# Attention visits of TensorE re-sequenced in a one-core decoder layer

## The chip, the cores and the metric

One core of one Trainium2 chip runs the whole layer. The time is device microseconds (us) of that core, from launch to end; smaller is better. The clock of TensorE has two levels, 1.2 and 2.4 GHz, and the profile gives the granted share of the higher one.

## The reference, cut to what matters

One layer on 512 tokens of width 1024: adaLN modulation of an RMSNorm, a mixture of three dilated sliding-window attentions with 16 heads of 64, a gated ConvFFN with a width-3 causal convolution, and a final RMSNorm.

```python
def reference(x, c, ...):
    mod = silu(c) @ w_ada + b_ada
    sh1, sc1, g1, sh2, sc2, g2 = split(mod, 6)
    h = rms_norm(x, norm_mix) * (1 + sc1) + sh1
    qkv = (h @ attn_w_in).reshape(B, S, 3, 3, 16, 64)        # q,k,v x groups x heads
    for g, (window, dilation) in enumerate(((128, 1), (512, 4), (2048, 16))):
        o, lse = dilated_window_attention(q[g], k[g], v[g], window, dilation)
    o = sum(softmax(lses over g) * outs)                     # a mixture per head
    x = x + g1 * (o @ attn_w_out)
    h = rms_norm(x, norm_ffn) * (1 + sc2) + sh2
    x = x + g2 * conv_ffn(h, w_up, conv_w, conv_b, w_down)
    return rms_norm(x, norm_final)
```

## The kernel before, in words

All large products are made in fp32r with operands split in a high and a low part (wh, wl for weights; hh, hl for the input): three matmuls of 128x512 for each 128 rows of contraction. ScalarE (ACT) makes the high part of a weight strip (L883), VectorE (DVE) the low part (L1131).

Attention goes by pairs of heads, of which there are 8. TensorE (PE) runs `body(n, par, project, attend)` nine times. With `project` it makes the nine q/k/v strips of pair n (L604 to L606), and with `attend` the attention of pair n-1. Body 0 only projects, bodies 1 to 7 do both (three rounds of a loop of two, and one more), body 8 only attends. A body has 18 half strips, h = 0 to 17, of 12 matmuls each; between them stand the visits to other work, at the h that a table gives:

- `make_scores` (L609) makes query-key products for a quarter d of the scores: side 0 (d = 0, 1) is the first group in windows of two blocks (L621), side 1 (d = 2, 3) the other two groups (L628). Contraction is over 64 rows, so head 0 uses the upper and head 1 the lower half of the array's rows, and the heads alternate matmul by matmul. Both heads write their own one of the two `score` banks. `mask_scores` on DVE (L1202) adds the mask, takes the maximum and moves them to `probs`, ACT exponentiates in place (L953).
- `turn_values` (L633) and `turn_probs` (L651) are transposes against the identity (L641, L657) into the two `turn` banks; DVE copies bank 0 out and ACT bank 1 (`take_turn`, L1192 and L923). `sum_ada` (L648) turns a partial sum of the modulation in bank 1 of the same pair; the counter `turn_taken` orders all of them.
- `weigh_values` (L661) makes the value products of one unit u: head u % 2 and quarter j = u // 2. Its weights are 64 columns wide, and head 0 writes partitions 0 to 63 of an output bank `o_acc[side]`, head 1 partitions 64 to 127. A visit makes a quarter: all of head 0's 6 or 8 matmuls, then all of head 1's (L676).

The tables put scores at h = 0, 2, 4, 6, the turned values at 3, 5, 7, the modulation sum at 10, the turned probabilities at 12, 14, 15, 16 and the value products at 14, 15, 16, 17. Between scores and probabilities DVE mixes the three groups' softmax denominators (h = 8, 9) and scales `probs` (`weigh`, L1218). At the end of a body ACT copies the output bank (L966), DVE adds the two (L1294), and ACT and DVE split the sum (L970, L1299).

In body 8 there is no projection; in its place PE begins the output projection (L684 to L686), `FILL_AT` giving the number of steps of three matmuls at each h. The last step of each of these four strips waits for the last pair's low part (L750). Then follow the rest of the output projection and the ConvFFN, which the change doesn't touch.

Of the kernel before, what the change touches and what calls it, by code (L numbers as in the profile page):

```python
# [25 lines left out]
P = 128  # L26
# [4 lines left out]
H, E = 16, 64  # L31
# [44 lines left out]
def decoder_layer(nc, x, c, w_ada, b_ada, norm_mix, norm_ffn, attn_w_in, attn_w_out,  # L76
# [11 lines left out]
    with ctx:  # L88
# [113 lines left out]
        turned = [sem("turned0"), sem("turned1")]  # L202
        turn_taken = [sem("turn_taken0"), sem("turn_taken1")]
# [18 lines left out]
        def turns_before(n):  # L222

            return 0 if isinstance(n, int) and n == 0 else 6 * n - 4


        SCORE_AT = {0: 0, 2: 1, 4: 2, 6: 3}
# [3 lines left out]
        TURN_P_AT = {12: 0, 14: 1, 15: 2, 16: 3}  # L231
        PV_AT = {14: 0, 15: 1, 16: 2, 17: 3}
# [7 lines left out]
        FILL_AT = {1: 3, 3: 3, 5: 3, 7: 10, 12: 3, 14: 1, 15: 1, 17: 4}  # L240
# [41 lines left out]
        def qkv_slot(n, s):  # L282
            return RING if is_first(n) and s == RING else s % RING

# [255 lines left out]
        def _(pe):  # L540
# [68 lines left out]
            def make_scores(n, par, d):  # L609
# [3 lines left out]
                pe.wait_ge(masked, 4 * (n - 1) + d + 1)  # L613
                side, tiles = d // 2, (2 * (d % 2), 2 * (d % 2) + 1)
                for b in tiles:
                    at = HALF * (b % 2)
                    if side == 0:
                        lo = P * max(b - 1, 0)
                        for hd in range(2):
                            e = slice(E * hd, E * (hd + 1))  # L620
                            last = nc.tensor.matmul(score[hd][:, at + (P if b == 0 else 0):at + HALF],  # L621
                                                    q_t[e, par, 0, P * b:P * (b + 1)],
                                                    k_t[e, par, 0, lo:P * (b + 1)], start=True, stop=True)
                    else:
                        for g in (1, 2):
                            for hd in range(2):
                                e = slice(E * hd, E * (hd + 1))
                                last = nc.tensor.matmul(score[hd][:, at + P * (g - 1):at + P * g],  # L628
# [874 lines left out]
```

## Time and profile before

| what | value |
|---|---|
| runs | 1020.44, 1021.26, 1022.64 us (median 1021.26) |
| profiled execution: span, first to last instruction | 1017.7 us |
| median of the runs less that span | 3.56 us |
| PE matmul busy | 973.8 us, 96% |
| DVE, ACT busy | 514.6 us (51%), 403.3 us (40%) |
| granted TensorE clock, mean | 0.988 |
| value products L676 | 480 matmuls, 47.1 us busy |
| scores L628, L621 | 384 matmuls, 35.1 us busy |
| turned probabilities L657 | 240, 33.0 us busy |

The profile is of one execution, and gives its span; what lies around it is known only as the distance to the median of the runs. A matmul's duration overlaps its neighbours' (the pipeline), so what a matmul costs PE is the distance from its start to the next one's start, which the timeline shows.

### The profile page before, as it was taken

The numbers are of one execution on the slowest core, as the hardware profiler recorded it, in microseconds if no ns is written. First come the engines' busy times: TensorE is split into PE (matmuls) and PEld (weight loads), VectorE is DVE, ScalarE is ACT, GpSimd is POOL, SyncE is SP. The second block draws the span as 40 slices with busy tenths as digits, with TensorE's granted clock in tenths as the row PEclk, the third lists the DMA queues.
The fourth block names the chain that finished last, engine by engine and source line by source line (L and its number), as shares of the span: only waits on it lengthen the run. The fifth ranks groups of instructions, "written<-read, shape, count | busy, mean of one in ns | idle before, by whom it ended". The sixth has DMA issues, their size and how long they took to land.

```text
span 1017.7 us, 14215 instructions
## 1 busy us (share of the span) xinstructions
PE 973.8 (96%) x5008; PEld 784.4 (77%) x5008; DVE 514.6 (51%) x1115; ACT 403.3 (40%) x721; POOL 31.3 (3%) x43
## 2 busy tenths in 40 slices
PE   4589999999999999999999989999999999999996
PEld 3478787887877878878778779888888888888885
DVE  5863663655735646357365557644444444412214
ACT  7433443434435344353443534633333333321212
POOL 3500000000000000000000000100000000000000
PEclk9699999999999999999999999999999999999999
DMA  9746341432324314333232203333333323232212
GB/s 310 210 116 194 112 133 48 125 118 90 95 89 123 124 41 124 124 103 124 62 114 74 62 22 90 100 101 91 95 97 89 102 83 103 83 104 86 99 62 83
DMA packets 151533, 106.94 MB, mean 105 GB/s; under 512 B 3510, under 2 KB 138830, under 8 KB 151502
## 3 DMA queue, kind: packets, MB, share of 16 engines
q1 hardware_dynamic: 151296, 106.45, 34.4%
q8 instruction: 19, 0.31, 0.1%
q14 instruction: 12, 0.10, 0.0%
q10 hardware_dynamic: 206, 0.08, 0.0%
HBM read 104.42 MB, written 2.10 MB: 105 GB/s over the span
## 4 chain that ended last, share of the span: by engine, by line
PE 92%; DVE 5%; ACT 1%; issue 1%; DMA 1%; SPq 0%; DVEq 0%; POOL 0%; ACTq 0%
PE bank L604 13%; PE bank L606 13%; PE bank L605 13%; PE bank L797 8%; PE bank L798 8%; PE bank L799 8%; PE bank L676 4%; PE bank L822 4%; PE bank L821 4%; PE bank L823 4%; PE bank L657 3%; PE bank L628 2%; PE bank L621 1%; DVE acc L1093 1%; PE bank L684 1%; PE bank L686 1%
## 5 line engine op out<-in xcount | busy, mean ns | idle before, releaser
L1131 DVE TENSOR_TENSOR wl<-raw,wh 128x1024 fp32r<-128x1024 f32 x144 | 177.4, 1232 | 305.1 <-ACT wh L883 304.6
L883 ACT ACTIVATE wh<-raw 128x1024 fp32r<-128x1024 f32 x144 | 152.2, 1059 | 200.8 <-PE bank L799 112.9
L604 PE MATMUL bank<-hh,wl 128*128 128x512 f32 x552 | 227.0, 411 | 0.0
L606 PE MATMUL bank<-hl,wh 128*128 128x512 f32 x552 | 218.7, 396 | 0.0
L605 PE MATMUL bank<-hh,wh 128*128 128x512 f32 x552 | 218.3, 395 | 0.0
L799 PE MATMUL bank<-fl,wh 128*128 128x512 f32 x336 | 133.0, 396 | 0.0
L798 PE MATMUL bank<-fh,wh 128*128 128x512 f32 x336 | 133.0, 396 | 0.0
L797 PE MATMUL bank<-fh,wl 128*128 128x512 f32 x336 | 133.0, 396 | 0.0
L604 PEld LDWEIGHTS bank<-hh,wl 128*128 128x128 f32 x552 | 104.1, 189 | 27.8 <-issue 5.7
L606 PEld LDWEIGHTS bank<-hl,wh 128*128 128x128 f32 x552 | 103.9, 188 | 24.7
L605 PEld LDWEIGHTS bank<-hh,wh 128*128 128x128 f32 x552 | 104.1, 189 | 20.7
L953 ACT ACTIVATE probs<-probs,nmax 128x256 f32<-128x256 f32 (+1 forms) x128 | 61.9, 485 | 98.4 <-DVE nmax L1208 98.4
L797 PEld LDWEIGHTS bank<-fh,wl 128*128 128x128 f32 x336 | 63.2, 188 | 15.3
L799 PEld LDWEIGHTS bank<-fl,wh 128*128 128x128 f32 x336 | 63.2, 188 | 15.2
L798 PEld LDWEIGHTS bank<-fh,wh 128*128 128x128 f32 x336 | 63.2, 188 | 15.1
L822 PE MATMUL bank<-act_h,wh 128*128 (+1 forms) x160 | 63.4, 396 | 0.0
L823 PE MATMUL bank<-act_l,wh 128*128 (+1 forms) x160 | 63.4, 396 | 0.0
L821 PE MATMUL bank<-act_h,wl 128*128 (+1 forms) x160 | 63.3, 396 | 0.0
L1192 DVE COPY p_t<-bank 128x512 f32<-128x512 f32 x32 | 22.1, 690 | 61.7 <-PE bank L657 61.7
L923 ACT ACTIVATE p_t<-bank 128x512 f32<-128x512 f32 x32 | 19.1, 598 | 79.4 <-PE bank L657 79.4
L676 PEld LDWEIGHTS bank<-p_t,v_n 128*64 128x64 f32 x480 | 39.4, 136 | 12.0 <-issue 10.7
L676 PE MATMUL bank<-p_t,v_n 128*64 128x128 f32 x480 | 47.1, 279 | 0.3 <-DVE p_t L1192 0.3
(175 smaller groups left out, 1147.7 us busy)
## 6 DMA issues: line engine op xcount, KB each, us to landing
raw<-in_attn_w_in SPq DMA_DIRECT2D x72, 512.0 KB, 3.8
raw<-in_ffn_w_up SPq DMA_DIRECT2D x44, 512.0 KB, 3.8
ada_raw<-in_w_ada SPq DMA_DIRECT2D x16, 1024.0 KB, 5.7
raw<-in_ffn_w_down SPq DMA_DIRECT2D x22, 512.0 KB, 3.3
ada<-in_w_ada SPq DMA_DIRECT2D x16, 256.0 KB, 7.1
raw<-in_attn_w_out SPq DMA_DIRECT2D x8, 512.0 KB, 3.6
x_nat<-in_x SPq DMA_DIRECT2D x4, 512.0 KB, 5.2
x_nat<-in_w_ada SPq DMA_DIRECT2D x8, 256.0 KB, 6.3
```

Source lines behind the costliest of these rows:

```text
L604: nc.tensor.matmul(bank[:], wl[:, slot, t], xh[:, t], start=(t == 0), stop=False)
L605: nc.tensor.matmul(bank[:], wh[:, slot, t], xh[:, t], start=False, stop=False)
L606: last = nc.tensor.matmul(bank[:], wh[:, slot, t], xl[:, t], start=False, stop=(t == KT - 1))
L676: last = nc.tensor.matmul(o_acc[side][e, P * b:P * (b + 1)], values, p_t[:, u % PT_RING, P * i:P * (i + 1)], start=first, stop=final)
L797: nc.tensor.matmul(bank[:], wl[:, slot, t], fh[:, t], start=(t == 0), stop=False)
L798: nc.tensor.matmul(bank[:], wh[:, slot, t], fh[:, t], start=False, stop=False)
L799: last = nc.tensor.matmul(bank[:], wh[:, slot, t], fl[:, t], start=False, stop=(t == KT - 1))
L821: nc.tensor.matmul(y[:], wl[:, slot, o], xh, start=start, stop=False)
L822: nc.tensor.matmul(y[:], wh[:, slot, o], xh, start=False, stop=False)
L823: last = nc.tensor.matmul(y[:], wh[:, slot, o], xl, start=False, stop=False)
L883: nc.scalar.activation(dst, src, ACT.Copy).then_inc(done, 1)
L1131: nc.vector.tensor_tensor(dst, src, high.bitcast(F32), ALU.subtract).then_inc(done, 1)
```

## The change

The scores of a side are made in one visit, its second quarter in the `turn` banks. Masks and exponentials get a table of their own (`MASK_AT`). The value products come in two visits, at h = 14 and 16, with the two heads alternating matmul by matmul. The probabilities of a side are turned in one visit over four banks (`turn` and `score`), in body 8 still quarter by quarter over two. The values are turned in the output banks. DVE scales the second half of `probs` at h = 11, ahead of its first copy of turned probabilities. The output steps in body 8 are spread anew, and each kind of turning has semaphores of its own.

```diff
-        SCORE_AT = {0: 0, 2: 1, 4: 2, 6: 3}
+        SCORE_AT = {0: (0, 1), 4: (2, 3)}
+        MASK_AT = {0: 0, 1: 1, 4: 2, 5: 3}
         TURN_V_AT = {3: 0, 5: 1, 7: 2}
         ADA_READ_AT = {0: 0, 1: 1, 2: 2, 3: 3, 5: 4, 6: 5, 7: 6, 8: 7}
         ADA_AT = 10
-        TURN_P_AT = {12: 0, 14: 1, 15: 2, 16: 3}
-        PV_AT = {14: 0, 15: 1, 16: 2, 17: 3}
+        TURN_P_AT = {12: (0, 1), 14: (2, 3)}
+        TURN_P_LAST = {12: (0,), 13: (1,), 14: (2,), 15: (3,)}
...
...
         def qkv_slot(n, s):
             return RING if is_first(n) and s == RING else s % RING
+        def score_bank(d, hd):
+            return (score, turn)[d % 2][hd]
+        def turn_bank(u, project):
...
                 if d == 0:
                     pe.wait_ge(strip_taken, STRIPS * n)
-                pe.wait_ge(masked, 4 * (n - 1) + d + 1)
+                if d == 1:
+                    pe.wait_ge(ada_taken, n)
...
-                            last = nc.tensor.matmul(score[hd][:, at + (P if b == 0 else 0):at + HALF],
+                            last = nc.tensor.matmul(score_bank(d, hd)[:, at + (P if b == 0 else 0):at + HALF],
...
             def turn_values(n, par, g):
                 k, use = g % 2, g // 2
                 pe.wait_ge(strip_taken, STRIPS * n + g + 1)
-                if not (isinstance(n, int) and n == 0 and use == 0):
-                    pe.wait_ge(turn_taken[k], turns_before(n) + use)
+                if use:
+                    pe.wait_ge(v_taken[0], 2 * n + 1)
+                elif not is_first(n):
+                    pe.wait_ge(o_summed, n)
                 src = v_t[:, (par + g) % 2]
                 for b in range(NT):
                     keys = src[:, P * b:P * (b + 1)] if g == 0 else src[:, b:T:4]
-                    last = nc.tensor.transpose(turn[k][:, P * b:P * (b + 1)], keys, ident[:])
-                last.then_inc(turned[k], 1)
+                    last = nc.tensor.transpose(o_acc[k][:, P * b:P * (b + 1)], keys, ident[:])
+                last.then_inc(v_turned[k], 1)
             def sum_ada(n):
                 pe.wait_ge(acc_step, KT * (n + 1))
-                pe.wait_ge(turn_taken[1], turns_before(n) + 1)
+                if not is_first(n):
+                    pe.wait_ge(masked, 4 * n)
                 for j in range(NT):
                     last = nc.tensor.transpose(turn[1][:, P * j:P * (j + 1)], acc[:, P * j:P * (j + 1)], ident[:])
-                last.then_inc(turned[1], 1)
-            def turn_probs(n, u, before):
-                hd, j, k = u % 2, u // 2, u % 2
+                last.then_inc(ada_turned, 1)
+            def turn_probs(n, u, project):
+                hd, j = u % 2, u // 2
                 pe.wait_ge(scaled, 8 * (n - 1) + u + 1)
-                pe.wait_ge(turn_taken[k], turns_before(n) + before + j)
+                if project and u == 1:
+                    pe.wait_ge(ada_taken, n + 1)
+                ring = 2 if project else 1
+                if j >= ring:
+                    pe.wait_ge(p_taken[hd], 4 * (n - 1) + j - ring + 1)
                 for i, (b, part) in enumerate(p_blocks(j)):
-                    last = nc.tensor.transpose(turn[k][:, P * i:P * (i + 1)],
+                    last = nc.tensor.transpose(turn_bank(u, project)[:, P * i:P * (i + 1)],
                                                probs[:, hd, j // 2, b, P * part:P * (part + 1)], ident[:])
-                last.then_inc(turned[k], 1)
-            def weigh_values(n, par, u, before):
-                hd, j, k = u % 2, u // 2, u % 2
-                e = slice(E * hd, E * (hd + 1))
-                pe.wait_ge(turn_taken[k], turns_before(n) + before + j + 1)
-                if u == 0:
+                last.then_inc(p_turned[hd], 1)
+            def weigh_values(n, par, j, project):
+                for hd in range(2):
+                    pe.wait_ge(p_taken[hd], 4 * (n - 1) + j + 1)
+                if j == 0:
                     pe.wait_ge(o_summed, n)
+                    if project:
+                        pe.wait_ge(v_taken[0], 2 * n + 2)
+                        pe.wait_ge(v_taken[1], n + 1)
                 side = j // 2
                 blocks = p_blocks(j)
                 for i, (b, part) in enumerate(blocks):
-                    if side == 0:
-                        values = v_n[:, par, 0, b - 1 + part, e]
-                    else:
-                        values = v_n[:, par, 1 + part, b, e]
                     first = i == 0 or blocks[i - 1][0] != b
                     final = i == len(blocks) - 1 or blocks[i + 1][0] != b
-                    last = nc.tensor.matmul(o_acc[side][e, P * b:P * (b + 1)], values, p_t[:, u % PT_RING, P * i:P * (i + 1)],
-                                            start=first, stop=final)
+                    for hd in range(2):
+                        e = slice(E * hd, E * (hd + 1))
+                        if side == 0:
+                            values = v_n[:, par, 0, b - 1 + part, e]
+                        else:
+                            values = v_n[:, par, 1 + part, b, e]
+                        last = nc.tensor.matmul(o_acc[side][e, P * b:P * (b + 1)], values,
+                                                p_t[:, (2 * j + hd) % PT_RING, P * i:P * (i + 1)],
+                                                start=first, stop=final)
...
-                            pe.wait_ge(masked, 4 * PAIRS + 1)
+                            pe.wait_ge(masked, 4 * PAIRS)
...
                         if h in SCORE_AT:
-                            make_scores(n, 1 - par, SCORE_AT[h])
-                        if h in PV_AT:
-                            for u in (2 * PV_AT[h], 2 * PV_AT[h] + 1):
-                                weigh_values(n, 1 - par, u, before)
-                        if h in TURN_P_AT:
-                            for u in (2 * TURN_P_AT[h], 2 * TURN_P_AT[h] + 1):
-                                turn_probs(n, u, before)
+                            for d in SCORE_AT[h]:
+                                make_scores(n, 1 - par, d)
+                        for j in PV_AT.get(h, ()):
+                            weigh_values(n, 1 - par, j, project)
+                        for j in (TURN_P_AT if project else TURN_P_LAST).get(h, ()):
+                            for u in (2 * j, 2 * j + 1):
+                                turn_probs(n, u, project)
                     if attend and not project and h in FILL_AT:
                         begin_out(fill_steps[filled:filled + FILL_AT[h]])
...
-            def take_turn(n, use, dst):
-                act.wait_ge(turned[1], turns_before(n) + use + 1)
-                nc.scalar.activation(dst, turn[1][:], ACT.Copy).then_inc(turn_taken[1], 1)
+            def take_probs(n, j, project):
+                act.wait_ge(p_turned[1], 4 * (n - 1) + j + 1)
+                u = 2 * j + 1
+                nc.scalar.activation(p_t[:, u % PT_RING], turn_bank(u, project)[:], ACT.Copy).then_inc(p_taken[1], 1)
...
                         if (TURN_V_FIRST if is_first(n) else TURN_V_AT).get(h) == 1:
-                            take_turn(n, 0, v_n[:, par, 1].rearrange("p b e -> p (b e)"))
+                            act.wait_ge(v_turned[1], n + 1)
+                            nc.scalar.activation(v_n[:, par, 1].rearrange("p b e -> p (b e)"), o_acc[1][:], ACT.Copy
+                                                 ).then_inc(v_taken[1], 1)
...
-                        if h in SCORE_AT:
-                            d = SCORE_AT[h]
+                        if h in MASK_AT:
+                            d = MASK_AT[h]
...
-                        if h in TURN_P_AT:
-                            u = 2 * TURN_P_AT[h] + 1
-                            take_turn(n, before + u // 2, p_t[:, u % PT_RING])
+                        for j in (TURN_P_AT if project else TURN_P_LAST).get(h, ()):
+                            take_probs(n, j, project)
...
-                    act.wait_ge(pv_done, 8 * n)
+                    act.wait_ge(pv_done, 4 * n)
...
-            def take_turn(n, use, dst):
-                dve.wait_ge(turned[0], turns_before(n) + use + 1)
-                nc.vector.tensor_copy(dst, turn[0][:]).then_inc(turn_taken[0], 1)
+            def take_values(n, g, dst):
+                dve.wait_ge(v_turned[0], 2 * n + g // 2 + 1)
+                nc.vector.tensor_copy(dst, o_acc[0][:]).then_inc(v_taken[0], 1)
+            def take_probs(n, j, project):
+                dve.wait_ge(p_turned[0], 4 * (n - 1) + j + 1)
+                u = 2 * j
+                nc.vector.tensor_copy(p_t[:, u % PT_RING], turn_bank(u, project)[:]).then_inc(p_taken[0], 1)
...
-                            probs[:, hd, side, b, lo:HALF], score[hd][:, HALF * (b % 2) + lo:HALF * (b % 2 + 1)],
+                            probs[:, hd, side, b, lo:HALF], score_bank(d, hd)[:, HALF * (b % 2) + lo:HALF * (b % 2 + 1)],
...
-                        if h in TURN_P_AT:
-                            u = 2 * TURN_P_AT[h]
-                            take_turn(n, before + u // 2, p_t[:, u % PT_RING])
-                            if u == 0:
-                                weigh(range(4, 8))
+                        if h == 11:
+                            weigh(range(4, 8))
+                        for j in (TURN_P_AT if project else TURN_P_LAST).get(h, ()):
+                            take_probs(n, j, project)
```

`before` and `turns_before` are gone everywhere; DVE's mask reads `score_bank(d, hd)`.

## Rows read from the trace of the kernel before

**Rows 1.** The page: busy time by engine, the chain of waits, groups of instructions.
```profile
PE 973.8 (96%) x5008; PEld 784.4 (77%) x5008; DVE 514.6 (51%) x1115; ACT 403.3 (40%) x721; POOL 31.3 (3%) x43
...
PE 92%; DVE 5%; ACT 1%; issue 1%; DMA 1%; SPq 0%; DVEq 0%; POOL 0%; ACTq 0%
...
L953 ACT ACTIVATE probs<-probs,nmax 128x256 f32<-128x256 f32 (+1 forms) x128 | 61.9, 485 | 98.4 <-DVE nmax L1208 98.4
```
**Rows 2.** Busy time by stretch: one body of the loop.
```profile
299.50:366.20 66.70, 66.70 (x373) 52.97 (x371) 36.22 (x102) 27.95 (x58) 0.00 (x0) 1.00 0.34 102
```
**Rows 3.** Waits, 233 to 560 us: waiter, releaser, total, times, longest.
```profile
DVE wl L1131 <- ACT wh L883: 73.8, 37, 3.4
...
PEld bank L676 <- issue: 7.0, 19, 0.4
```
**Rows 4.** Timeline of PE: start, length, form, count; one score visit.
```profile
256.93 0.40 PE L606 MATMUL bank<-hl,wh 128*128 128x512 f32 x1
257.25 1.16 PE L628 MATMUL bank<-k_t,q_t 64*128 64x128 f32 x16
258.35 0.50 PE L604 MATMUL bank<-hh,wl 128*128 128x512 f32 x1
258.68 0.40 PE L605 MATMUL bank<-hh,wh 128*128 128x512 f32 x1
```
**Rows 5.** Timeline of PE: value products and turned probabilities, same body.
```profile
282.50 1.15 PE L676 MATMUL bank<-p_t,v_n 128*64 128x128 f32 x12
283.58 1.09 PE L657 MATMUL bank<-ident,probs 128*128 128x128 f32 x8
...
287.07 0.40 PE L606 MATMUL bank<-hl,wh 128*128 128x512 f32 x1
287.39 1.58 PE L676 MATMUL bank<-p_t,v_n 128*64 128x128 f32 x16
288.91 1.09 PE L657 MATMUL bank<-ident,probs 128*128 128x128 f32 x8
...
290.07 0.39 PE L605 MATMUL bank<-hh,wh 128*128 128x512 f32 x1
...
297.73 0.40 PE L606 MATMUL bank<-hl,wh 128*128 128x512 f32 x1
298.06 1.58 PE L676 MATMUL bank<-p_t,v_n 128*64 128x128 f32 x16
...
299.91 0.39 PE L605 MATMUL bank<-hh,wh 128*128 128x512 f32 x1
```
**Rows 6.** The visit at 287.39: matmuls in flight 287.60 to 287.87, and 287.9 to 288.3.
```profile
287.39 0.65 PE L676 MATMUL bank<-p_t,v_n 128*64 128x128 f32 x4
...
287.66 0.88 PE L676 MATMUL bank<-p_t,v_n 128*64 128x128 f32 x10
```
**Rows 7.** Timeline of PE in body 8.
```profile
564.16 0.40 PE L606 MATMUL bank<-hl,wh 128*128 128x512 f32 x1
...
566.00 0.93 PE L621 MATMUL bank<-k_t,q_t 64*128 64x128 f32 x8
...
587.13 1.01 PE L657 MATMUL bank<-ident,probs 128*128 128x128 f32 x6 [2.04 <-DVE probs L1218]
...
603.56 0.46 PE L684 MATMUL bank<-oh,wl 128*128 128x512 f32 x1
```
**Rows 8.** Timeline of ACT and DVE in body 8.
```profile
564.59 1.07 ACT L940 ACTIVATE k_t<-bank 128x512 f32<-128x512 f32 x1 [1.25 <-PE bank L606]
...
569.96 0.17 DVE L1208 TENSOR_SCALAR nmax<-stat 128x4 f32<-128x4 f32 x1
...
581.91 2.81 DVE L1258 COPY swap<-stat 32x8 f32<-32x8 f32 x16 [2.15 <-ACT probs L953]
...
586.52 2.06 DVE L1218 TENSOR_SCALAR probs<-probs,mix 128x128 f32<-128x128 f32 x8
...
589.10 2.19 DVE L1218 TENSOR_SCALAR probs<-probs,mix 128x256 f32<-128x256 f32 x8
...
602.78 0.69 DVE L1299 TENSOR_TENSOR ol<-o_sum,oh 128x512 fp32r<-128x512 f32 x1 [0.70 <-ACT oh L970]
```
**Rows 9.** Timeline of ACT and DVE, second strip split of a loop body.
```profile
242.78 1.04 ACT L883 ACTIVATE wh<-raw 128x1024 fp32r<-128x1024 f32 x1
...
276.73 0.69 DVE L1192 COPY p_t<-bank 128x512 f32<-128x512 f32 x1
```

More of the change, by code:

```diff
@@ L201, in decoder_layer @@
         y_done = sem("y_done")
-        turned = [sem("turned0"), sem("turned1")]
-        turn_taken = [sem("turn_taken0"), sem("turn_taken1")]
+        v_turned, v_taken = [sem("v_turned0"), sem("v_turned1")], [sem("v_taken0"), sem("v_taken1")]
+        ada_turned, ada_taken = sem("ada_turned"), sem("ada_taken")
+        p_turned, p_taken = [sem("p_turned0"), sem("p_turned1")], [sem("p_taken0"), sem("p_taken1")]
         scored, masked, nmax_done, exp_done = sem("scored"), sem("masked"), sem("nmax_done"), sem("exp_done")
@@ L237, in decoder_layer @@
         ADA_FIRST = 17
-        FILL_AT = {1: 3, 3: 3, 5: 3, 7: 10, 12: 3, 14: 1, 15: 1, 17: 4}
+        FILL_AT = {0: 5, 4: 15, 12: 1, 13: 1, 14: 1, 15: 1, 16: 4}
         OUT_AHEAD = 4
@@ L283, in qkv_slot @@
             return RING if is_first(n) and s == RING else s % RING
+        def score_bank(d, hd):
+            return (score, turn)[d % 2][hd]
+        def turn_bank(u, project):
+            return (turn + score)[u % 4] if project else turn[u % 2]
         def split_at(n, h):
@@ L612, in make_scores @@
                     pe.wait_ge(strip_taken, STRIPS * n)
-                pe.wait_ge(masked, 4 * (n - 1) + d + 1)
+                if d == 1:
+                    pe.wait_ge(ada_taken, n)
+                if d >= 2:
+                    pe.wait_ge(masked, 4 * (n - 1) + d - 1)
                 side, tiles = d // 2, (2 * (d % 2), 2 * (d % 2) + 1)
@@ L627, in make_scores @@
                                 e = slice(E * hd, E * (hd + 1))
-                                last = nc.tensor.matmul(score[hd][:, at + P * (g - 1):at + P * g],
+                                last = nc.tensor.matmul(score_bank(d, hd)[:, at + P * (g - 1):at + P * g],
                                                         q_t[e, par, g, P * b:P * (b + 1)],
@@ L716, in body @@
             def body(n, par, project, attend):
-                before = 2 if project else 0
                 filled = 0
@@ L919, in _ @@
                 start_high(c)
-            def take_turn(n, use, dst):
-                act.wait_ge(turned[1], turns_before(n) + use + 1)
-                nc.scalar.activation(dst, turn[1][:], ACT.Copy).then_inc(turn_taken[1], 1)
+            def take_probs(n, j, project):
+                act.wait_ge(p_turned[1], 4 * (n - 1) + j + 1)
+                u = 2 * j + 1
+                nc.scalar.activation(p_t[:, u % PT_RING], turn_bank(u, project)[:], ACT.Copy).then_inc(p_taken[1], 1)
             def body(n, par, project, attend):
-                before = 2 if project else 0
                 for h in range(HALVES):
@@ L936, in body @@
                             if is_first(n) and s == 2:
-                                act.wait_ge(turned[0], 1)
+                                act.wait_ge(v_turned[0], 1)
                             dst = {"v": v_t[:, (par + g) % 2], "q": q_t[:, par, g], "k": k_t[:, par, g]}[kind]
@@ L1221, in body @@
             def body(n, par, project, attend):
-                before = 2 if project else 0
                 for h in range(HALVES):
@@ L1241, in body @@
                         if h == (ADA_FIRST if is_first(n) else ADA_AT):
-                            dve.wait_ge(turned[1], turns_before(n) + 2)
+                            dve.wait_ge(ada_turned, n + 1)
                             nc.vector.tensor_reduce(mod_raw[:, bass.ds(MOD1 + NT * n, NT)],
                                                     turn[1][:].rearrange("p (t n) -> p t n", n=P), AX.X, ALU.add
-                                                    ).then_inc(turn_taken[1], 1)
+                                                    ).then_inc(ada_taken, 1)
                         g = (TURN_V_FIRST if is_first(n) else TURN_V_AT).get(h)
                         if g in (0, 2):
-                            take_turn(n, g // 2, v_n[:, par, g].rearrange("p b e -> p (b e)"))
+                            take_values(n, g, v_n[:, par, g].rearrange("p b e -> p (b e)"))
                     if attend:
-                        if h in SCORE_AT:
-                            mask_scores(n, SCORE_AT[h])
+                        if h in MASK_AT:
+                            mask_scores(n, MASK_AT[h])
                         if h == 8:
@@ L1302, in _ @@
             bodies(dve, body)
-            dve.wait_ge(turn_taken[1], turns_before(PAIRS - 1) + 2)
+            dve.wait_ge(ada_taken, PAIRS)
             nc.vector.tensor_tensor(mod[:, MOD1:MOD], mod_raw[:, MOD1:MOD], cols_a[:, MOD1:MOD], ALU.add
```

6 lines of the change are left out of this document (2 added, 4 removed).

## The prediction

> **What bounds the kernel now.** The page first: PE is busy for 96% of the span and the chain of waits that ended last is 92% PE [rows 1]. So a change counts by what it does to PE's order of starts. Then the windows: one body of the attention loop lasts 66.70 us, PE is busy in all of it at a granted clock of 1.00 (the 2.4 GHz level), while DVE has 36.22 and ACT 27.95 us [rows 2]. Then the waits of bodies 1 to 6: the long ones are DVE's and ACT's; for PE's weight loads only "issue" stands, the gap on entering a visit of another form, 7.0 us in 19 times before L676 [rows 3]. No engine makes PE wait in the loop. The seven bodies that project and attend are thus priced by PE's start-to-start distances, and body 8 by following its chain.
>
> **Distances.** Four projection matmuls, L606 at 256.93, the visit, L604 at 258.35, L605 at 258.68, give the price of a visit: from the L606 to the L605 are 1.75 us, of which two projection matmuls take 0.467 (0.233 each: 216 of them are 50.4 of the 66.70). So 16 score matmuls cost 1.28 us [rows 4]. They run in pairs of heads. A single stream of 128-column matmuls goes at 0.109: of the 1.09 us of eight turned probabilities 0.27 is the last one's own length, and the first gap behind value products is longer [rows 5]. Eight pairs at 0.109 are 0.87, so 0.41 of the 1.28 is fixed: entry, a long first gap, exit.
>
> **Scores in one visit.** Two visits become one twice in a body; the matmuls stay. One fixed part of 0.41 goes; pairs run nearer to 0.112, so I take 0.40. Bounds: nothing (if the four banks bring a pause between quarters as long as the one removed) and 0.41. 2 x 0.40 = 0.80 us a body.
>
> **Value products, heads alternating.** Now, by the same sum as for the scores: at 287.07 the visit and the eight turned probabilities behind it take 3.00 - 0.467 = 2.53, less 8 x 0.109 = 0.87, so 1.67. The one at 298.06, behind which projection follows, 2.18 - 0.467 = 1.71. The small one of 12 lasts 1.08 from start to start against 1.52 of the one of 16, so 1.67 - 0.44 = 1.23. Sum 1.23 + 1.67 + 1.67 + 1.71 = 6.28 us a body [rows 5]. Within a visit the first four starts lie over 0.65 - 0.27 = 0.38 (0.16, then 0.109 twice), but ten later ones over 0.88 - 0.27 = 0.61, nine gaps of 0.068 [rows 6]. There the second head's stream has begun beside the first's; its first start lies near the first head's sixth, and both ends of the visit are one head alone. So the two column halves do run side by side, each at 0.109. After the change there are 14 pairs at h = 14 and 16 at h = 16. With 0.109 a pair and a fixed part of 0.41 less 0.05 (the first gap is 0.16, against 0.21 from 257.25 to the next pair, for which 8 pairs in 1.10 leave room) and less 0.04 more where transposes follow: 0.32 + 1.53 = 1.85 and 0.36 + 1.74 = 2.10, together 3.95. Gain 6.28 - 3.95 = 2.33. Bounds of the pair: 0.109 (the score rows; nothing faster is seen) and 0.218 (the heads one after the other): gain between 2.33 and about -0.9. I take 0.109, since row 6 shows the very halves overlapping.
>
> The Trainium skill, "TensorE: Matmul & The Clock Gate", Part 3, speaks against this: weight loads overlap matmuls in flight only where the row group differs, and matmuls start in strict program order. Both heads' value products use all rows. By that rule the heads would go one after the other, the 0.218 case. The trace disagrees on the order: with strictly ordered starts at 0.109, ten matmuls would need 0.98 us, and they take 0.61 [rows 6].
>
> **Turned probabilities and values, masks.** The 30 + 12 + 4 transposes of a body are the same, and a visit of them costs no more than its matmuls, so their regrouping is nothing; between -0.1 and 0.1. V in the output banks adds a wait for `o_summed` at h = 3, four halves after the sum's end: nothing. The value products at h = 14 wait for copies whose sources PE turned at the end of h = 12, two halves (5.6 us) earlier; the two DVE copies are 1.4 us. DVE's second scaling (2.19 us) now stands ahead of the first copy, which before started at 276.73 [rows 8, 9]; a first copy near 277.5 and a second by 279 leave 3 us to spare. On ACT the first two exponential visits now follow one another (4 x 0.49 = 1.96 us each, L953 [rows 1]), and the strip split behind them moves from 242.78 [rows 9] to about 246; its strip is used at h = 6, near 255. Queued behind it are the SP load of the same raw slot and DVE's low part, which keep over 5 us. If that cover were gone, each us late would be a us of each body. The mask of d = 1 is done some 10 us before the scores at h = 4 ask for it. So nothing here.
>
> A body gains 0.80 + 2.33 = 3.13 us (66.70 to about 63.6), seven bodies 21.9.
>
> **Body 8**, from its last L606 at 564.16 to the last output step's first matmul at 603.56: 39.40 us, with the value visit of body 7 (1.71, counted above) inside [rows 7]. After, on the same clock: that visit is gone from h = 17, so the scores arrive before ACT's copy of the last k strip (564.59, 1.07 long [rows 8]) and wait to 565.7, a new wait of 1.3. Both quarters 1.7, five output steps 3.6: 571.0. DVE, whose output sum no longer waits for value products, has the first quarter's maximum at 569.6 (0.4 before the 569.96 of now [rows 8]), splits a strip (1.2), and has the second at 572.2. So d = 3 starts at 572.3, and output steps run from 573.35 over 15 x 0.70: 583.95. The second exponentials begin at 572.5, three visits of 1.96 end at 578.5 (581.9 now); the mixing chain is 587.13 - 581.91 = 5.22 long, so the first probabilities are scaled at 583.7, just in time: the 2.04 wait [rows 7] goes. But in this body the second quarter can be turned only when DVE has copied the first, and DVE's 2.19 of scaling is ahead of that copy: 583.1 + 2.06 + 2.19 + 0.69 = 588.05, against PE's arrival at 585.4. This is the new late thing, 2.65 us. From there: eight transposes and an output step, then the wait for ACT's copy: 589.85; 14 pairs to 591.5; transposes and step 593.2; the same 594.9; 16 pairs to 596.9; four steps to 599.8. The last low part comes 2.7 us + 0.69 after the last value product now (602.78 [rows 8]); in the new order it ends near 599.8 too. 599.85 - 564.16 = 35.7, 3.7 less, minus the 1.7 counted: 2.0 us. Bounds 0 (two more copies late, 1 us each) and 3.1 (all its PE work saved).
>
> **Sum.** 21.9 + 2.0 = 23.9. Span 1017.7 - 23.9 = 993.8. The median of the runs lies 3.56 above the profiled span, so 1021.26 - 23.9 = 997.4 us. What comes after moves along.
>
> **The rivals.**
> (a) Waits eat part: ACT's or DVE's regrouped work reaches PE in each body. For it: exponentials back to back, two copies in a row, scaling before copying. Against: the spare times above. At 1 us in each of seven bodies 1004.4.
> (b) The heads don't run side by side when strictly alternated (the rule above, as a mechanism: one weight load at a time for all rows). Value visits 28 and 32 single steps of 0.109 + 0.68 = 7.22, 0.94 more than now; less 0.80: 0.14 a body worse. About 1022, no change. For it: only that the trace has no strictly alternating column halves. Against: rows 6.
> (c) Slower: each change of column half costs the long gap of a visit's first matmul, 0.16 instead of 0.109, with no overlap. 60 x 0.16 + 0.6 = 10.2, 3.9 more, less 0.80: 3.1 a body, seven bodies and body 8 about 24 us: 1045. It decides from a pair distance of 0.23 up, where 26 further pair gaps eat the 3.13. For it: the first gap of each form is long. Against: score pairs, whose halves change at each matmul, at 0.11.
> (d) Better: switching is dearer than the fixed part shows, or body 8 saves its full 3.1 and more: 994 to 995.
>
> **Chances.** Forecast 0.76 (alone 995 to 1000.5), (a) 0.12, (b) 0.04, (c) 0.03, (d) 0.05. The range 994.5 to 1003.5 holds the forecast, (d) and two thirds of (a), about 0.85, less what I don't see. A measurement here tells apart from about 0.2%, 2 us. Faster: forecast, (a), (d): 0.93; same 0.04; slower 0.03.
>
> **What would show it.** Right: loop bodies of 63.4 to 63.8 us; L676 in two groups a body, x28 in about 1.85 and x32 in 2.1 us, starts two by two; score groups of 16 (side 0) and 32; no PE wait on another engine in the loop; in body 8 one PE wait of 2 to 3 us before a turned quarter, released by DVE's copy, and one of about 1.3 before the scores, by ACT's k strip. Wrong: L676 starts evenly 0.109 apart (b) or 0.16 (c); PE idle on strips, copies or exponentials in each body (a). A changed time after the attention, where nothing was altered, would be outside all of this.

## The result, and the profile after

The changed kernel takes 995.45 us (median of four runs, 995.13 to 998.02); the kernel before, on the same chip, took 1021.34. The ratio is 0.9751, with a 95% interval of 0.9734 to 0.9768: faster by about 2.5%. The forecast was 997.4, range 994.5 to 1003.5. The profiled span is 993.8 us; the forecast for the span was 1017.7 - 23.9 = 993.8. Between the medians the gain is 25.9 us, between the two profiled spans 23.9; the account below is of the spans.

The page of the changed kernel (columns as in [rows 1]): PE has 26.3 us less of busy time with the same 5008 matmul records, and the chain that ended last is still PE's.

```profile
PE 947.5 (95%) x5008; PEld 772.0 (78%) x5008; DVE 512.5 (52%) x1115; ACT 403.0 (41%) x721; POOL 31.3 (3%) x43
...
PE 90%; DVE 6%; ACT 2%; issue 1%; DMA 1%; SPq 0%; DVEq 0%; POOL 0%; ACTq 0%
...
L976 ACT ACTIVATE probs<-probs,nmax 128x256 f32<-128x256 f32 (+1 forms) x128 | 61.9, 485 | 64.7 <-DVE nmax L1234 64.7
```

Busy time by stretch of the changed kernel, one body of the loop and then body 8 from its last projection matmul to the first matmul of the last output step. The body answers to [rows 2]: 66.70 has become 63.50, PE still busy in all of it at a granted clock of 1.00. (The 66.70 was cut 0.09 too long: counted from visit to visit, as all bodies below are where no window is shown, it is 66.61 before and 63.49 after, in each of the six distances between value visits.) Body 8 was 39.40 [rows 7] and is 35.11.

```profile
222.45:285.95 63.50, 63.50 (x372) 51.62 (x371) 35.67 (x103) 29.14 (x59) 0.00 (x0) 1.00 0.36 107
544.48:579.59 35.11, 31.44 (x224) 24.96 (x223) 20.80 (x86) 15.56 (x44) 0.00 (x0) 1.00 0.08 25
```

Timeline of PE in the same body: the score visit of 32 matmuls [rows 4], then the two value visits [rows 5].

```profile
243.35 0.40 PE L612 MATMUL bank<-hl,wh 128*128 128x512 f32 x1
243.68 2.06 PE L637 MATMUL bank<-k_t,q_t 64*128 64x128 f32 x32
245.67 0.50 PE L610 MATMUL bank<-hh,wl 128*128 128x512 f32 x1
246.00 0.40 PE L611 MATMUL bank<-hh,wh 128*128 128x512 f32 x1
...
276.44 0.40 PE L612 MATMUL bank<-hl,wh 128*128 128x512 f32 x1
276.77 1.75 PE L697 MATMUL bank<-p_t,v_n 128*64 128x128 f32 x28
278.45 1.97 PE L673 MATMUL bank<-ident,probs 128*128 128x128 f32 x16
280.17 0.48 PE L610 MATMUL bank<-hh,wl 128*128 128x512 f32 x1
280.49 0.40 PE L611 MATMUL bank<-hh,wh 128*128 128x512 f32 x1
...
285.62 0.40 PE L612 MATMUL bank<-hl,wh 128*128 128x512 f32 x1
285.95 1.97 PE L697 MATMUL bank<-p_t,v_n 128*64 128x128 f32 x32
287.85 0.50 PE L610 MATMUL bank<-hh,wl 128*128 128x512 f32 x1
288.18 0.39 PE L611 MATMUL bank<-hh,wh 128*128 128x512 f32 x1
```

Read as before: the score visit costs 246.00 - 243.35 - 0.467 = 2.18 us (forecast 1.28 + 1.28 - 0.40 = 2.16). The value visit before projection costs 288.18 - 285.62 - 0.467 = 2.09 (forecast 2.10). The one before 16 transposes costs 280.49 - 276.44 - 0.467 - 16 x 0.109 = 1.84 (forecast 1.85).

Waits of the changed kernel in the loop, 225 to 540 us (waiter, releaser, total, times, longest), to set beside [rows 3]. None of the waiting lines is PE's on another engine. DVE's wait for the DMA of the modulation weights has grown, from 0.2 us in one place to 11.9 in five; no PE wait followed from it. PE's entry gap ahead of value products came 19 times before and comes 10 times now.

```profile
DVE wl L1153 <- ACT wh L904: 74.4, 22, 4.5
...
DVE acc L1263 <- DMA ada_raw<-in_w_ada: 11.9, 5, 3.1
...
PEld bank L697 <- issue: 3.7, 10, 0.4
```

PE's waits on other engines in the changed kernel, 540 to 600 us; the first two lie in body 8, the third behind it (the kernel before has it there too):

```profile
PE bank L673 <- DVE p_t L1218: 2.5, 1, 2.5
PE bank L630 <- ACT k_t L961: 1.1, 1, 1.1
PE bank L706 <- DVE wl L1153: 0.4, 1, 0.4
```

And the timeline of ACT, PE and DVE behind the first two: the copy of the last k strip, the scores, DVE's second scaling ahead of its first copy, then the second copy (an answer to [rows 8]).

```profile
544.91 1.04 ACT L961 ACTIVATE k_t<-bank 128x512 f32<-128x512 f32 x1 [4.80 <-PE bank L612]
546.00 1.79 PE L630 MATMUL bank<-k_t,q_t 64*128 64x128 f32 x16 [1.13 <-ACT k_t L961]
...
563.21 4.16 DVE L1244 TENSOR_SCALAR probs<-probs,mix 128x128 f32<-128x128 f32 x16
567.28 0.69 DVE L1218 COPY p_t<-bank 128x512 f32<-128x512 f32 x1
568.78 0.69 DVE L1218 COPY p_t<-bank 128x512 f32<-128x512 f32 x1 [0.81 <-PE bank L673]
```

**Where the 23.9 us of span come from.** The first scores start at 103.15 us, 0.40 later than before (102.75). From there to the last projection matmul it is 441.33 us instead of 461.41: 20.1 saved. Body 8 gives 39.40 - 35.11 = 4.3. Behind the attention the rest is the same to 0.05 us (414.12 and 414.16). 20.1 + 4.3 - 0.4 = 24.0, which is the 23.9 to rounding.

### The profile page after: what moved, and what is told of

The parts are those of the page before. It is cut to its first block, busy times and chain, and to the rows that moved or that the text cites. A ratio compares the mean times of both kernels' runs of the same rounds, so it can differ in the third digit from the quotient of the medians.

```text
span 993.8 us, 14153 instructions
## 1 busy us (share of the span) xinstructions
PE 947.5 (95%) x5008; PEld 772.0 (78%) x5008; DVE 512.5 (52%) x1115; ACT 403.0 (41%) x721; POOL 31.3 (3%) x43
## 4 chain that ended last, share of the span: by engine, by line
PE 90%; DVE 6%; ACT 2%; issue 1%; DMA 1%; SPq 0%; DVEq 0%; POOL 0%; ACTq 0%
PE bank L610 13%; PE bank L612 13%; PE bank L611 13%; PE bank L818 8%; PE bank L819 8%; PE bank L820 8%; PE bank L844 4%; PE bank L843 4%; PE bank L842 4%; PE bank L697 3%; PE bank L673 3%; DVE acc L1115 1%; PE bank L637 1%; PE bank L630 1%; PE bank L652 1%; PE bank L706 1%
## 5 line engine op out<-in xcount | busy, mean ns | idle before, releaser
L610 PE MATMUL bank<-hh,wl 128*128 128x512 f32 x552 | 224.2, 406 | 0.0
L610 PEld LDWEIGHTS bank<-hh,wl 128*128 128x128 f32 x552 | 104.0, 188 | 26.3 <-issue 3.5
L1263 DVE SCALAR_TENSOR_TENSOR acc<-ada_raw,cond,acc 128x512 f32<-128x512 f32 x56 | 42.0, 749 | 15.2 <-DMA ada_raw<-in_w_ada 14.5
L961 ACT ACTIVATE k_t<-bank 128x512 f32<-128x512 f32 x24 | 22.1, 922 | 65.9 <-PE bank L612 65.9
L1228 DVE CUSTOM_DVE_ANT_0 probs<-bank,mask 128x256 f32<-128x256 f32 (+1 forms) x128 | 44.4, 403 | 5.5 <-PE bank L637 5.5
L961 ACT ACTIVATE q_t<-bank 128x512 f32<-128x512 f32 x24 | 26.9, 1119 | 47.3 <-PE bank L612 47.3
```

The lines of the kernel that those rows point to most:

```text
L610: nc.tensor.matmul(bank[:], wl[:, slot, t], xh[:, t], start=(t == 0), stop=False)
```

## Experiments

My theory: the value products gain because two column halves run side by side when their matmuls are close in PE's order, the scores gain one fixed part a visit, and DVE's scaling ahead of a short copy is the one new late thing in body 8. The rivals: the gain is only fewer visits (then alternation is worth nothing), or it comes from the exponentials and copies arriving otherwise. Beside each time stand the body of the loop (63.50 in the changed kernel) and body 8 as measured above (35.11). The kernel before ran beside them in 1021.56, 1021.46 and 1021.75 us. Edits are against the changed kernel unless said otherwise.

**Heads one after the other in each quarter**, still two visits.

```diff
-                for i, (b, part) in enumerate(blocks):
-                    ...
-                    for hd in range(2):
+                for hd in range(2):
+                    for i, (b, part) in enumerate(blocks):
+                        ...
```

> The changed kernel, but within a quarter all value products of head 0 come before those of head 1, as before the change; still two visits a body. Theory (the column halves overlap only near a change of head, about 3.5 of 16 matmuls, as in the old visits): each of the three changes of head in a visit overlaps 3.5, so 17.5 and 21.5 steps of 0.109 us instead of 14 and 16, 1.0 us a body, 8 us in all: 1003. If only the change from head 0 to head 1 overlaps: 1.7 us a body, 1009. Rival (the gain came from having fewer visits, not from the alternation): 996.

Measured: 1005.26 us, ratio 0.9853 (0.9825 to 0.9881), span 1003.2. The body, and its value visit of 32:

```profile
225.61:290.18 64.57, 64.57 (x372) 52.69 (x371) 35.66 (x102) 29.12 (x59) 0.00 (x0) 1.00 0.35 105
...
287.88 2.57 PE L697 MATMUL bank<-p_t,v_n 128*64 128x128 f32 x32
```

The body is 1.08 longer than 63.49, the visit 0.60 (2.57 against 1.97). (2.57 - 0.32) / 0.109 + 1 is 21.6 steps of 0.109 where pairs need 16: with heads in turn only the matmuls near a change of head overlap. The time is 2 us above the forecast of 1003: body 8 is 37.74, 2.6 longer than in the changed kernel. By estimate 1.0 of that is the edit, as in a loop body, and the other 1.6 came with the granted clock, which fell to 0.50 behind PE's 2.5 us wait (see the last section).

**Alternation alone**: the kernel before, with its four value visits and its score visits, only the heads alternating.

```diff
-                for i, (b, part) in enumerate(blocks):
-                    ...
-                    last = nc.tensor.matmul(o_acc[side][e, P * b:P * (b + 1)], values, p_t[:, u % PT_RING, P * i:P * (i + 1)],
+                for i, (b, part) in enumerate(blocks):
+                    for hd in range(2):
+                        ...
+                        last = nc.tensor.matmul(o_acc[side][e, P * b:P * (b + 1)], values,
+                                                p_t[:, (2 * j + hd) % PT_RING, P * i:P * (i + 1)],
```

> The kernel before, with one edit: in each of the four value visits the heads alternate. Theory: 30 pairs x 0.109 + three times 0.32 + 0.36 = 4.6 us a body against 6.28, 1.7 less, eight bodies 13 us: 1008. Rival (visits count, not the alternation): 1021. Rival (alternation needs the new order to be of use): between.

Measured: 1008.1 us, ratio 0.9879 (0.9852 to 0.9906), span 1006.3.

```profile
167.68:232.57 64.89, 64.89 (x371) 51.15 (x370) 36.24 (x103) 27.91 (x59) 0.00 (x0) 1.00 0.35 106
...
223.72 1.09 PE L677 MATMUL bank<-p_t,v_n 128*64 128x128 f32 x16
```

A value visit of 16 lasts 1.09 us where it lasted 1.58 [rows 5], and a body is 1.72 shorter (66.61 to 64.89). More than half of the body's 3.12 is alternation and nothing else: that the gain is only fewer visits is refuted. What is left, 3.12 - 1.72 - 0.80 for the scores = 0.60, fits two value visits fewer at the 0.29 that the run with one value visit below measures for each.

**Four score visits again**, in the loop bodies.

```diff
-        SCORE_AT = {0: (0, 1), 4: (2, 3)}
-        MASK_AT = {0: 0, 1: 1, 4: 2, 5: 3}
+        SCORE_AT = {0: (0,), 2: (1,), 4: (2,), 6: (3,)}
+        MASK_AT = {0: 0, 2: 1, 4: 2, 6: 3}
```

> The changed kernel with four score visits (h = 0, 2, 4, 6) and their masks in bodies 1 to 7, body 8 as changed. Theory: two fixed parts of 0.40 us come back in each of seven bodies, 5.6 us: 1001. Rival (joining score visits is worth nothing): 995.5.

Measured: 1003.51 us (1000.72 to 1004.8), ratio 0.9831 (0.9806 to 0.9855), span 998.9.

```profile
230.96:295.26 64.30, 64.28 (x371) 51.42 (x370) 35.70 (x102) 28.91 (x60) 0.00 (x0) 1.00 0.35 106
```

The body is 0.80 longer, two fixed parts of 0.40, as the prediction had it (four of the six distances; two are 1.02 longer, and why is open). The first scores started 0.8 earlier than in the changed kernel, which is why the span is only 5.1 longer, where 7 x 0.80 = 5.6 and two times 0.2 were due. The median lies 8 us above that of the changed kernel. The profiled run was the fastest of the four, and the 3 us between it and the median no trace shows.

**All of one head, then all of the other**, over both quarters of a visit.

```diff
-                for i, (b, part) in enumerate(blocks):
-                    for hd in range(2):
+                for hd in range(2):
+                    for j in js:
+                        for i, (b, part) in enumerate(p_blocks(j)):
```

The visit now waits at its start for the copies of both its quarters; no wait of PE in the loop came of it.

> The changed kernel, but in a visit all 14 or 16 value products of head 0 come first, then all of head 1. Theory (overtaking reaches only a few matmuls ahead): one overlap of 3.5 a visit, 24.5 and 28.5 steps, 2.5 us a body more, 20 us in all: 1015. If PE could start the other head's work however far behind it stands in the order: 996. Between the two, the distance from the first head-1 start to the last head-0 start gives the reach.

Measured: 1017.25 us (ten runs, 1014.99 to 1019.45), ratio 0.9962 (0.9947 to 0.9977), span 1013.7. Body 65.98, 2.49 longer; body 8 37.80. The body, its value visit of 32, and the matmuls in flight at the start of that visit (291.86 to 293.1) and at 293.5, where the heads change:

```profile
228.94:294.92 65.98, 65.98 (x373) 54.10 (x371) 35.66 (x102) 29.13 (x59) 0.00 (x0) 1.00 0.34 103
...
291.86 3.33 PE L697 MATMUL bank<-p_t,v_n 128*64 128x128 f32 x32
...
291.86 1.42 PE L697 MATMUL bank<-p_t,v_n 128*64 128x128 f32 x11
...
293.23 0.59 PE L697 MATMUL bank<-p_t,v_n 128*64 128x128 f32 x6
```

Alone, a stream goes at (1.42 - 0.27 - 0.05) / 10 = 0.11 us; where the heads meet, six starts lie within 0.59 - 0.27 = 0.32, five gaps of 0.064. The visit comes to (3.33 - 0.32) / 0.109 + 1 = 28.6 steps. If the second head's stream started only when the first had ended it would be 32; if it ran beside it from the start, 16. 28.6 says that its first matmul starts with the one that has three of the first head's behind it, and the starts fit: counted back from the visit's last start at 294.92, the second head's first is at 294.92 - 0.05 - 15 x 0.109 = 293.23, while the first head's last is at 291.86 + 0.05 + 15 x 0.109 = 293.55. So the side-by-side reaches past three matmul instructions and no further, and this alone, with the same visits as in the changed kernel, gives back 2.5 of the 3.12 us of a body. By the rule of the Trainium skill, "TensorE: Matmul & The Clock Gate", Part 3, that matmuls start in strict program order, the second head's first matmul could start with the last of the first head at the earliest: 31 steps here, and 29 with the heads in turn in each quarter. The runs have 28.6 and 21.6, so by this measurement the rule doesn't hold for two column halves. The strictly alternating order is no test of it, since 16 steps need no overtaking; they speak against rival (b), one head's weights at a time.

**Two and two**: four matmul instructions of one head, then four of the other.

```diff
-                for i, (b, part) in enumerate(blocks):
-                    for hd in range(2):
+                for tile in (2 * (j % 2), 2 * (j % 2) + 1):
+                    here = [(i, part) for i, (b, part) in enumerate(blocks) if b == tile]
+                    for hd in range(2):
+                        for i, part in here:
```

> The changed kernel with coarser alternation: two value products of head 0, then two of head 1 (each product is two matmul instructions in the trace, so groups of four instead of two). Theory (from the visit ordered by head: head 1's first matmul started together with the one that has three of head 0's behind it): groups of four still pair fully, a loop body stays 63.5 us; 995.5. Rival (only strict alternation pairs): each group loses one to two steps of 0.109, 15 groups a body, 1.6 to 3 us a body, 1008 or more.

Measured: 997.45 us (997.42 to 998.34), ratio 0.9773 (0.9753 to 0.9793), span 995.7. One row for the body, two for PE in body 8 (busy, granted clock, DMA share, GB/s):

```profile
229.94:293.54 63.60, 63.60 (x372) 1.00 0.35 107
...
569.00:571.00 2.00, 2.00 (x14) 0.69 0.00 0
571.00:573.00 2.00, 2.00 (x23) 0.50 0.04 8
```

The body is 63.60: four in a row still pair, at a price of 0.11 us a body. That fits the reach that the last run showed. Body 8 is 36.77, 1.7 longer than 35.11, and not by this edit: PE's clock fell to 0.50, the 1.2 GHz level, behind the 2.5 us wait for DVE's copy, which this kernel has too. With it the 2 us between 997.45 and 995.45 are accounted for; the change of grain itself is worth 0.8 in the loop (7 x 0.11).

**Copy before scaling in body 8.**

```diff
-                        if h == 11:
+                        if h == 11 and project:
                             weigh(range(4, 8))
                         for j in (TURN_P_AT if project else TURN_P_LAST).get(h, ()):
                             take_probs(n, j, project)
+                        if h == 13 and not project:
+                            weigh(range(4, 8))
```

> The changed kernel, but in body 8 DVE scales the second half of the probabilities after the first two copies of turned probabilities, no longer ahead of them. Theory (the 2.5 us wait of PE before the second turned quarter is DVE's 2.19 us of scaling standing in front of its copy): that wait shrinks to about 0.7 and the first value visit of body 8 starts 1.9 us earlier; 993.6. Rival (the chain behind it is as long anyway, so the wait moves to the next copy): 995.4.

Measured: 993.12 us (992.56 to 995.17), ratio 0.9731 (0.9708 to 0.9753), span 990.8, body 8 33.00. PE's wait, and DVE's timeline around it:

```profile
PE bank L673 <- DVE p_t L1218: 0.5, 1, 0.5
...
564.36 0.69 DVE L1218 COPY p_t<-bank 128x512 f32<-128x512 f32 x1
565.86 0.69 DVE L1218 COPY p_t<-bank 128x512 f32<-128x512 f32 x1 [0.81 <-PE bank L673]
566.47 1.66 DVE L1244 TENSOR_SCALAR probs<-probs,mix 128x256 f32<-128x256 f32 x6
```

The 0.69 us copy no longer stands behind the scaling; the wait falls from 2.5 to 0.5 and body 8 by 2.1. That the new late thing was the order on DVE, not the turning or the exponentials, is shown.

**One value visit in a body.** The four extra units of turned probabilities go where nothing is kept at that time.

```diff
-        PV_AT = {14: (0, 1), 16: (2, 3)}
+        PV_AT = {16: (0, 1, 2, 3)}
+        PV_LAST = {14: (0, 1), 16: (2, 3)}
...
+        def p_unit(u):
...
+            return p_t[:, u] if u < PT_RING else (v_t[:, 0], v_t[:, 1], acc[:], o_a[:])[u - PT_RING]
```

> The changed kernel with the two value visits of bodies 1 to 7 made one at h = 16: the four units of turned probabilities that the ring has no room for go to tiles idle at that time. Theory (a visit's fixed part is 0.3 to 0.4 us whatever its length, and 60 matmuls run as 30 pairs of 0.109): L697 in one group of x60, 2.45 us less 0.33 a body, 2.3 us in all: 993.1. Rival (a waited-for copy of 16 matmuls' transposes, two halves earlier, or the o_a and v_t tiles hold ACT or DVE back): 995.4 or above.

Measured: 995.21 us (994.74 to 996.86), ratio 0.9748 (0.9726 to 0.977), span 993.1. The body, and PE in body 8 around its 2.6 us wait:

```profile
229.40:292.60 63.20, 63.20 (x371) 1.00 0.36 108
...
562.40:565.90 3.50, 0.96 (x6) 1.00 0.00 0
566.00:568.50 2.50, 2.50 (x11) 0.50 0.00 0
```

The body gained 0.29 (forecast 0.33), 2.0 over seven. The forecast of the whole missed: body 8, which the edit does not touch, is 36.68 instead of 35.11, since the clock came back at 0.50 after the wait and stayed there for about three microseconds. That took 1.6 back.

**Two output steps before the scores in body 8**, to hide the 1.1 us wait for ACT's k strip.

```diff
+                    if attend and not project and h == 0:
+                        begin_out(fill_steps[0:2])
+                        filled = 2
```

(and two steps fewer at h = 4)

> The changed kernel, but in body 8 two of the output steps stand ahead of the first scores, taken from the thirteen... fifteen behind the second scores. Theory (body 8 is bound by the chain mask, exponentials, mixing, scaling; PE's 1.1 us wait for the last k strip is cover that this chain gives back): that wait goes, and PE waits as much more before the first turned probabilities; 995.4, no change within 0.3. Rival (PE's own work bounds this part): 1.1 to 1.4 less, 994.2.

Measured: 997.62 us (995.54 to 999.52), ratio 0.9763 (0.9738 to 0.9788), span 996.7, body 8 35.27. PE's wait for the k strip is gone, but this one came in its place:

```profile
566.87 1.00 PE L673 MATMUL bank<-ident,probs 128*128 128x128 f32 x6 [1.03 <-DVE probs L1247]
```

Body 8 is as long as before: the chain through maximum, exponentials, mixing and scaling starts with the scores, which start no earlier, and PE's work ahead of them only moves its wait. The span's extra 2.9 us arise before the first scores (106.04 instead of 103.15), which this edit cannot touch.

**Both good edits** (copy before scaling, one value visit), to see whether they add and whether the clock stays up once the wait is short.

```diff
+        PV_AT = {16: (0, 1, 2, 3)}
...
+                        if h == 13 and not project:
+                            weigh(range(4, 8))
```

> The changed kernel with the copy order of body 8 and the single value visit of bodies 1 to 7 together, body 8 otherwise as changed. Theory: in the run with the single visit alone the clock was granted at half after PE's 2.6 us wait in body 8 and cost 1.6 us; with the wait cut to 0.5 it stays up, so both gains count: body 8 33.0 us from the last projection matmul to the last output steps, loop bodies 63.2; 2.1 + 2.0 less than the changed kernel, 991.3. Rival (the clock falls in that stretch whatever the wait): 993.

Measured: 991.08 us (990.45 to 993.04), ratio 0.971 (0.9692 to 0.9729), span 989.5, body 8 32.99; one row for the body, one for PE behind the wait, and the wait:

```profile
229.39:292.59 63.20, 63.20 (x372) 1.00 0.36 108
...
565.00:567.00 2.00, 2.00 (x31) 1.00 0.00 0
...
PE bank L678 <- DVE p_t L1223: 0.4, 1, 0.4
```

They add (2.0 and 2.1 of the 993.8 - 989.5 = 4.3), the clock stays at 1.00, and this has the lowest median, 4.4 us below the changed kernel.

**All of it, and the chain of body 8 shortened**: the two edits, two output steps before the scores, the masks of the first quarters ahead of the low part of the output sum on DVE, and a strip split moved behind them on ACT and DVE.

```diff
-                    if attend and not project and h == 0:
+                    if attend and not project and h == 4:
                         split_out(split_h, 3, h_ready, wh)
...
-                    if attend and not project and h == 0:
+                    if attend and not project and h == 1:
+                        low_sum(PAIRS - 1)
+                    if attend and not project and h == 5:
                         split_out(split_l, 3, l_ready, wl)
```

> Both edits of the copy order and of the single value visit, and body 8 with its chain shortened: DVE takes the masks of the first two quarters before the low part of the last output sum, the split of the fourth output strip moves from h = 0 to h = 4 and 5, and two of the first five output steps stand ahead of the scores. Theory: 1.9 from the copy, 2.3 from the visits, 1.3 from the chain, 5.5 together: 989.9. Rival (in body 8 only one of them counts, since each shortens the same chain): 991.5 to 993.

Measured: 992.17 us (990.51 to 993.74), ratio 0.9714 (0.9691 to 0.9737), span 991.0, body 63.20, body 8 31.95. Body 8 is 1.04 us shorter than with the two edits alone, the shortest of all; but the first scores start at 105.65, 2.5 later than in the changed kernel, and eat it. Against the kernel of the two edits its median is not told apart: the intervals overlap.

## Why the prediction was right

- **What bounds the kernel.** PE's start distances in the loop, as said: neither the changed kernel nor any of its variants has a PE wait on another engine in the loop, and each edit of the changed kernel there moved the stretch from the first scores to the last projection matmul by seven times its body's difference, to within 0.5 us.
- **Scores, 0.80 a body.** Measured 0.80 by undoing it (in two of six bodies 1.02).
- **Value products, 2.33 a body.** 3.12 less 0.80 is 2.32, and the two visits cost 1.84 and 2.09 where 1.85 and 2.10 were forecast. The choice of 0.109 a pair rested on [rows 6], ten starts in 0.61 us, and that reading held, but for one step: the second head starts with the first head's fifth matmul of eight (three behind it), where the prediction said near the sixth. The prediction's words "heads alternating" left out one thing: each product shows as two matmul instructions, so the changed kernel alternates by two, and what matters is that no more than three instructions of one head stand ahead of the other's next.
- **Masks, exponentials, copies, V in the output banks: nothing.** No PE wait came in the loop; rival (a) did not happen.
- **Body 8.** Forecast: a new wait of 1.3 before the scores (measured 1.1, ACT's k strip), the 2.04 wait gone (gone), a new wait of 2.65 for DVE's copy (measured 2.5), 35.7 in all (measured 35.11). The 0.6 too much is spread over the whole of it: 0.2 by the end of the second scores, 0.3 by the end of the first value visit, 0.5 by the end of the second; no single step explains it.
- **The sum.** From the first scores to the last projection matmul 21.9 - 1.7 = 20.2 forecast, 20.1 measured; body 8 3.7 and 4.3. The 0.6 too much in body 8 met the 0.4 us that the start took, so the exact hit of the span is partly luck.
- **From span to median.** The prediction put the median 3.56 us above the span, the distance of one profile; here it is 1.65. This is nearly all of the 1.95 between 997.4 and 995.45, and it is the term that was furthest off. Every run on record, of every kernel, took 1.7 to 1.8 us more than its own span. The other 1.8 of the 3.56 is only that the profiled execution of the kernel before was that much faster than the median of its runs. That part belonged in the range, not in the sum; what made the other executions slower no trace shows.
- **The rivals.** (a) did not happen in the loop. (b) and (c) are refuted by pairs at 0.109 (a visit of 32 in 1.97 us); (d) asked for switching dearer than 0.41 or body 8 at its full 3.1, and body 8 went half of that way. The prediction says that the range from 994.5 holds (d), but half of (d)'s 994 to 995 lies below it; and from 0.109 a pair, 3.13 us over the 28 gaps between pairs in two visits is reached at 0.22, not 0.23. Neither changes the forecast.

## What to carry to other kernels

Price a change on a bound PE by start-to-start distances, visit by visit, and look inside one visit for matmuls that start closer than one stream allows: there the engine already shows what a finer interleave of independent halves is worth. Take a wait away only if what it waits for is on the chain that ends last; otherwise, as with the output steps before the scores, it comes back a few microseconds later. Never let microseconds of long work on a helper engine stand ahead of the short copy that the bound engine needs next: that order was worth 2.1 us here; and in some runs the clock fell behind such a wait, which cost a further 1.6.

## What the runs showed of the hardware

- **Reach of the side-by-side.** Two column halves pair up when at most three matmul instructions of one half that haven't started stand ahead of the other half's next; beyond this one stream goes alone at 0.109 us a matmul of 128 columns. Orders by 2, by 4, by quarter (6 or 8 instructions of a head) and by visit (14 or 16) gave bodies of 63.50, 63.60, 64.57 and 65.98 us. Why the reach is three was not tried.
- **The clock behind a wait.** Seven profiles have the PE wait of 2.5 to 2.6 us in body 8. In three (heads in turn, two and two, one value visit) the granted clock fell to 0.50 after it, at a cost of about 1.6 us; in four (the changed kernel, four score visits, visit by head, steps before the scores) it stayed at 1.00 on the same wait. In the three with a wait of 0.4 to 0.5 it never fell. A wait of 2.0 has both outcomes too: with it the clock stayed at 1.00 in the kernel before, and in the kernel before with alternation alone it was 0.63 and then 0.52 in the four microseconds from 576. So the length of the wait alone does not decide, and what does is open; for the changed kernel these two rows, PE in its wait and after it, show that the clock stayed:

```profile
564.70:568.10 3.40, 0.88 (x5) 1.00 0.00 0
568.10:570.00 1.90, 1.89 (x15) 1.00 0.00 0
```

- **The start varies.** The first scores start between 102.3 and 106.0 us in kernels that are nearly alike up to there. In the two that started latest, at 105.65 and 106.04, the granted clock from 45 to 60 us, where PE waits much, was 0.67 and 0.68. In the other ten, which start between 102.3 and 103.2, it was 0.79 to 0.89, and there a higher clock goes with no earlier start (0.81 before and 0.89 after, which started 0.40 later). That the low clock made the two late is likely and not shown. A start that moves the end by 3 us limits what single profiles tell; it is why bodies, and not whole times, are compared above.
